# A two-block transformer kernel: modulation accumulations at the end of a feed-forward step, statistic sums shared by POOL and TensorE, a table square root, and the branch scaled on VectorE

## What is computed

```python
def rms_norm(x, g):
    y = x * lax.rsqrt(jnp.mean(x * x, axis=-1, keepdims=True) + EPS)
    return y * g
def modulate(x, g, shift, scale):
    return rms_norm(x, g) * (1 + scale[:, None]) + shift[:, None]
def swiglu(h, w13, w2):
    a, b = jnp.split(h @ w13, 2, axis=-1)
    return (jax.nn.silu(a) * b) @ w2

# first block, layer l: nine modulation vectors from one product
mod = silu(c) @ ada_w[l] + ada_b[l]            # ada_w: [1024, 9 * 1024]
sh1, sc1, g1, sh2, sc2, g2, sh3, sc3, g3 = jnp.split(mod, N_ADA, axis=-1)
h = modulate(x, norm_g[l, 0], sh1, sc1)
x = x + 0.5 * g1[:, None] * swiglu(h, ff_w13[l, 0], ff_w2[l, 0])
...                                            # mixer (hybrid, then NSA), second half feed-forward
# after both layers: rms_norm(x, final_g)

# second block, layer i: a norm before and after each branch
h = rmsnorm(x, g_pre)
f = (silu(h @ w_gate) * (h @ w_up)) @ w_down
x = x + 0.5 * rmsnorm(f, g_post)               # twice; between them
x = x + rmsnorm(mixer(rmsnorm(x, mix_pre)), mix_post)   # conformer convolution, then differential attention
```

## Time and profile before

| | us |
|---|---|
| median of 3 runs | 2526.31 |
| lowest, highest | 2525.79, 2539.52 |
| the profiled execution | 2526.72 |
| its span (first to last instruction) | 2524.9 |
| mean granted TensorE clock | 0.932 of full speed |

### The profile page before, as it was taken

How to read it: one execution, slowest core, us unless ns; L and a number is a source line. 1 busy time by engine, 2 the same in 40 slices (tenths; PEclk the granted TensorE clock), 3 DMA queues, 4 the chain that set the end, 5 groups by cost and what they waited for, 6 DMA issues and landing times.

```text
span 2524.9 us, 41719 instructions
## 1 busy us (share of the span) xinstructions
PE 2252.9 (89%) x17470; PEld 2207.7 (87%) x17470; DVE 1547.4 (61%) x2128; ACT 946.2 (37%) x1209; POOL 113.2 (4%) x68
## 2 busy tenths in 40 slices
PE   2999868898899988989999997978998998987998
PEld 2999868898899988979998997868998998977998
DVE  7666675666766653656447555976556555575654
ACT  2333423333333344433334334224334333434433
POOL 0000000000000000000000001630000000000000
PEclk9999889899999987989998998988998998998999
DMA  6466533466556533114544552213453553411552
GB/s 275 196 256 257 207 139 134 175 250 257 203 227 261 226 137 132 50 51 184 183 167 152 183 182 100 101 40 143 173 192 120 200 183 133 159 59 67 200 182 83
DMA packets 52942, 417.58 MB, mean 165 GB/s; under 512 B 5873, under 2 KB 6001, under 8 KB 6769
## 3 DMA queue, kind: packets, MB, share of 16 engines
q1 hardware_dynamic: 52848, 416.27, 43.9%
HBM read 415.20 MB, written 1.05 MB: 165 GB/s over the span
## 4 chain that ended last, share of the span: by engine, by line
PE 59%; DVE 20%; DMA 10%; ACT 5%; issue 4%; POOL 1%; SPq 1%; DVEq 0%; ACTq 0%
PE AB L259 10%; PE AB L261 10%; PE AB L260 10%; DMA raw<-slabs 10%; DVE ada_acc L1357 7%; PE Y L259 6%; PE Y L260 6%; PE Y L261 6%; DVE lo L1328 4%; ACT hi L954 4%; DVE qT L1903 2%; PE M L524 2%; PE Y L721 2%; PE Y L736 1%; PE M L752 1%
## 5 line engine op out<-in xcount | busy, mean ns | idle before, releaser
L1328 DVE TENSOR_TENSOR lo<-raw,hi 128x2048 fp32r<-128x2048 f32 x322 | 748.5, 2326 | 632.5 <-ACT hi L954 632.3
L259 PE MATMUL AB<-h_hi,hi 128*128 128x256 f32 x3072 | 880.7, 287 | 12.6 <-DVE ada_raw L1913 5.8
L260 PE MATMUL AB<-h_lo,hi 128*128 128x256 f32 x3072 | 875.1, 285 | 0.0
L261 PE MATMUL AB<-h_hi,lo 128*128 128x256 f32 x3072 | 874.8, 285 | 0.0
L954 ACT ACTIVATE hi<-raw 128x2048 fp32r<-128x2048 f32 x322 | 614.6, 1910 | 645.3 <-DMA raw<-slabs 249.2
L259 PEld LDWEIGHTS AB<-h_hi,hi 128*128 128x128 f32 x3072 | 595.8, 194 | 15.3 <-DVE ada_raw L1913 6.8
L260 PEld LDWEIGHTS AB<-h_lo,hi 128*128 128x128 f32 x3072 | 595.9, 194 | 0.1
L261 PEld LDWEIGHTS AB<-h_hi,lo 128*128 128x128 f32 x3072 | 595.4, 194 | 0.0
L259 PE MATMUL Y<-g_hi,hi 128*128 128x256 f32 x1280 | 372.8, 291 | 53.0 <-DVE g_lo L1535 53.0
L261 PE MATMUL Y<-g_hi,lo 128*128 128x256 f32 x1280 | 370.4, 289 | 0.0
L260 PE MATMUL Y<-g_lo,hi 128*128 128x256 f32 x1280 | 370.3, 289 | 0.0
(11 more groups left out here) (291 smaller groups left out, 2274.7 us busy)
## 6 DMA issues: line engine op xcount, KB each, us to landing
raw<-slabs SPq DMA_DIRECT2D x322, 1024.0 KB, 4.8
ada_raw<-ada SPq DMA_DIRECT2D x35, 2048.0 KB, 7.8
x<-x_t SPq DMA_DIRECT2D x1, 1024.0 KB, 10.1
kT<-ada SPq DMA_DIRECT2D x1, 1024.0 KB, 18.4
vt<-ada SPq DMA_DIRECT2D x1, 1024.0 KB, 20.4
out_t<-x SPq DMA_DIRECT2D x4, 256.0 KB, 2.4
vec<-vectors SPq DMA_DIRECT2D x1, 462.0 KB, 3.5
hf<-constants SPq DMA_DIRECT2D x1, 401.0 KB, 15.1
```

Source lines behind the costliest of these rows:

```text
L259: nc.tensor.matmul(out_, w_hi, r_hi, start=start, stop=False, **kw)
L260: nc.tensor.matmul(out_, w_hi, r_lo, start=False, stop=False, **kw)
L261: return nc.tensor.matmul(out_, w_lo, r_hi, start=False, stop=stop, **kw)
L1328: nc.vector.tensor_tensor(lo[slot][:, :], raw[slot][:, :], hi[slot][:, :].bitcast(F32), ALU.subtract).then_inc(lo_done[slot], 1)
```

## The change

Four edits:

1. In VectorE's `step` of a feed-forward, `mod_out` moves behind `gate_lo`, and `mac` becomes the last instruction group of the step, behind the split of A. The order of SP, ScalarE and TensorE in the loop stays.
2. `tree` on POOL makes three additions instead of four; TensorE's `stat_tree` sums chunks 4 and 5 itself and takes them first.
3. A new `deviation` on ScalarE takes `sqrt(M + eps)` with the activation table, and `root_of_sqrt` on VectorE takes its reciprocal and one Newton step. It serves norms 1 to 5, 7 and 10, the final norm and the six additions of the second block. `sqrt_table` runs a small square root on ScalarE at the end of every feed-forward and mixer, before the slabs of `ahead()`.
4. `add(n)` for n >= 6: ScalarE only squares; VectorE scales the branch from PSUM into `hf`, before it takes the root.

```diff
@@ VectorE, step of a feed-forward
                     if not first:
                         split(sb_, i + nb)
+                    split(sw, i + nw)
+                    gate_lo(i + (g0 - 1))
                     if out_:
                         mod_out(i + (q0 - 2))
+                    if a:
+                        split(sa, i + (na + 1))
                     if mac_:
                         mac(0, i + (q0 - 1), i + (a0 - 1))
-                    split(sw, i + nw)
-                    gate_lo(i + (g0 - 1))
-                    if a:
-                        split(sa, i + (na + 1))
@@ TensorE, stat_tree
-                s0, p0 = c.take("sq", KD), c.take("pair", 4)
-                sums([(pair_ready, p0 + 3, sq[:, 0, :]), (pair_ready, p0 + 4, sq[:, 4, :]),
-                      (sq_ready, s0 + 7, sq[:, 6, :]), (sq_ready, s0 + 8, sq[:, 7, :])], ones[1024])
+                s0, p0 = c.take("sq", KD), c.take("pair", 3)
+                sums([(sq_ready, s0 + 5, sq[:, 4, :]), (sq_ready, s0 + 6, sq[:, 5, :]),
+                      (pair_ready, p0 + 3, sq[:, 0, :]), (sq_ready, s0 + 7, sq[:, 6, :]),
+                      (sq_ready, s0 + 8, sq[:, 7, :])], ones[1024])
@@ POOL, tree
-                pool.wait_ge(sq_ready, s0 + 6)
-                nc.gpsimd.tensor_tensor(sq[:, 4, :], sq[:, 4, :], sq[:, 5, :], ALU.add).then_inc(pair_ready, 1)
@@ ScalarE
+            def deviation():
+
+                act.wait_ge(stat_ready, c.take("stat") + 1)
+                nc.scalar.activation(root[:, :], M[:, 0:TT], ACT.Sqrt, bias=eps_[:, 0:1]).then_inc(sqrt_ready, 1)
+
+            def sqrt_table():
+
+                nc.scalar.activation(eps_[:, 1:2], eps_[:, 0:1], ACT.Sqrt)
...
                 g_split(g0 + NSTEP - 1, z_hi)
+                if f >= 4:
+                    c.take("stat")
+                sqrt_table()
                 ahead()
@@ ScalarE, add(n), n >= 6
                             nc.scalar.activation(ysq[:, k, :], Y[:, k, :], ACT.Square, bias=bias).then_inc(sq_ready, 1)
-                        if b == 0:
-                            act.wait_ge(gate_done, n - 5)
-                        for k in (2 * b, 2 * b + 1):
-                            if n == 7:
-                                nc.scalar.activation(hf[:, k, :], Y[:, k, :], ACT.Identity, scale=gate[:, k:k + 1],
-                                                     bias=gate_bias[:, k:k + 1]).then_inc(yg_ready, 1)
-                            else:
-                                nc.scalar.activation(hf[:, k, :], Y[:, k, :], ACT.Copy, scale=gate[:, k:k + 1]
-                                                     ).then_inc(yg_ready, 1)
+                    deviation()
@@ VectorE
+            def root_of_sqrt():
+
+                c.take("stat")
+                vh, tmp = var[:, 0:TT], var[:, TT:2 * TT]
+                dve.wait_ge(sqrt_ready, c.take("sqrt") + 1)
+                nc.vector.tensor_scalar(vh, M[:, 0:TT], EPS, -0.5, ALU.add, ALU.mult).then_inc(dve_link, 1)
+                c.take("link")
+                link(nc.vector.reciprocal(root[:, :], root[:, :]))
+                for t in range(TT):
+                    y = root[:, t:t + 1]
+                    nc.vector.scalar_tensor_tensor(tmp[:, t:t + 1], y, y, vh[:, t:t + 1], ALU.mult, ALU.mult
+                                                   ).then_inc(dve_link, 1)
+                at = c.take("link", TT)
+                for t in range(TT):
+                    y = root[:, t:t + 1]
+                    dve.wait_ge(dve_link, at + t + 1)
+                    nc.vector.scalar_tensor_tensor(y, tmp[:, t:t + 1], 1.5, y, ALU.add, ALU.mult
+                                                   ).then_inc(root_ready, 1)
+                dve.wait_ge(rstd_ready, c["stat"])
@@ VectorE, add(n), n >= 6
-                rstd_of(EPS, copy=False)
                 yg0 = (n - 6) * KD
+                for k in range(KD):
+                    if k % 2 == 0:
+                        dve.wait_ge(sq_ready, SQ_DONE["add", n] - KD + k + 2)
+                    nc.vector.tensor_scalar(hf[:, k, :], Y[:, k, :], gate[:, k:k + 1],
+                                            gate_bias[:, k:k + 1] if n == 7 else None, ALU.mult,
+                                            *([ALU.add] if n == 7 else [])).then_inc(yg_ready, 1)
+                root_of_sqrt()
```

More of the change, by code:

```diff
@@ L146, in program @@
         gate_bias = sb("gate_bias", [P, KD])
+        eps_ = sb("eps", [P, 2])
         ident = sb("ident", [P, P])
@@ L224, in program @@
         o_read = sem("o_read")
-        gate_done = sem("gate_done")
+        sqrt_ready = sem("sqrt_ready")
         yg_ready = sem("yg_ready")
@@ L289, in program @@
                 n_sq += 3
-            if kind == "norm":
-                SQ_DONE[a[0]] = n_sq
+            if kind == "norm" or kind == "add" and a[0] >= 6:
+                SQ_DONE[kind, a[0]] = n_sq
         ADA_FFN = {0: (4, 10), 1: (16, 10), 2: (26, 8), 3: (34, 2)}
@@ L1194, in hybrid @@
                 turn(4, first=4)
+                c.take("stat", 2)
+                sqrt_table()
                 next_slab()
@@ L1368, in begin @@
                 nc.vector.memset(one[:, :], 1.0)
+                nc.vector.memset(eps_[:, :], EPS)
                 for n, t in ones.items():
@@ L1472, in square_sum @@
             def square_sum(n):
-                dve.wait_ge(sq_ready, SQ_DONE[n])
+                dve.wait_ge(sq_ready, SQ_DONE["norm", n])
                 nc.vector.tensor_reduce(rstd[:, :], hf[:, :, :].rearrange("p k t -> p t k"), AXX, ALU.add
@@ L1603, in add @@
                     link(nc.vector.tensor_scalar(gate[:, :], g_src, half, None, ALU.mult))
-                    nc.vector.tensor_tensor(gate_bias[:, :], gate[:, :], v("b_pw2", 0, KD), ALU.mult
-                                            ).then_inc(gate_done, 1)
-                elif n >= 6:
-                    nc.vector.tensor_scalar(gate[:, :], g_src, half, None, ALU.mult).then_inc(gate_done, 1)
+                    link(nc.vector.tensor_tensor(gate_bias[:, :], gate[:, :], v("b_pw2", 0, KD), ALU.mult))
                 else:
```

1 line of the change is left out of this document (added).

## The result

The changed kernel takes 2645.74 us (median; 2642.75 to 2646.7) where the kernel before takes 2526.05 us in runs on the same chip: ratio 1.046, 95% interval 1.042 to 1.049, +119.7 us. The forecast was 2629 us, +102. The profiled execution took 2646.12 us, with a span of 2642.9 us, 118.0 us more than the span of 2524.9 us before.

A forecast was written before the change was run, and what follows sets the result against it. The kernel was taken to be bound in its coupled feed-forward steps by a ring from VectorE's accumulation over SP's loads and the splits. 2526.7 us +132 for the longer ring -30 for the statistics = 2629 us, range 2605 to 2655.

The forecast's parts named there:

- The ring: Coupled feed-forward steps: accumulation, ada_raw issue, slab loads behind it, splits, next accumulation; the move adds 132 us over four feed-forwards.
- The period's terms: Coupled step: 20.5 us plus W's split 2.2, gate_lo 0.6, A's split 2.2, wait 0.3, sequencer 0.1 makes 25.9 us.
- B lands E+10.2: Coupled step: the load of slab B lands 10.2 us after E, the end of an accumulation.
- 0.3 us for `hi` of W: Coupled step: VectorE waits 0.3 us for ScalarE's hi of slab W, counted into the longer period.
- A comes in time, 0.4 us to spare: Coupled step: ScalarE has slab A split by E+17.3, VectorE wants it at E+17.7; a later hi would show it wrong.
- First shift 5.9 us: Start of each feed-forward: the first accumulation comes 5.9 us later, behind W, gate_lo and A.
- Way out -2.5 us: End of each feed-forward's coupled steps: the last part gives back 2.5 us, bounds -4 and 0.
- The statistics: Norms and six additions: root 14.7, tree 5.6 and branch scaling 10.6 less 1.4 for table loads save 30 us, bounds 15 to 40.
- The early table loads: ScalarE's added loads, 1.28 us each, lie where it waits for TensorE; cost 1.4 us; one on the chain would show it wrong.
- the third rival: ScalarE's 16 added table loads lie uncovered, adding 20 us: 2649 us; chance 9%.
- the low clock would hold through the holes: Coupled steps: TensorE's waits keep it at the lower clock, 31.7 us a period, 2741 us in all; chance 4%.
- the ring keeps its length: Coupled steps: some slack takes the added 5.4 us, so only the statistics count: 2497 us; chance 3%.

The follow-up runs named there:

- e1: The kernel before with edit 1 alone (accumulation last in VectorE's step, mod_out behind gate_lo): 2667.16 us, ratio 1.055.
- e3: The changed kernel with SP issuing a step's ada_raw load behind the next step's three slab loads: 2424.78 us, ratio 0.959.
- e2: The changed kernel with VectorE's old order in the step, so edits 2 to 4 alone: 2509.16 us, ratio 0.992.
- e6: The changed kernel without its calls of sqrt_table, so each root loads its table itself: 2637.5 us, ratio 1.042.
- e11: The kernel of e2 (edits 2 to 4 alone) run once more: 2499.39 us, ratio 0.987.
- e10: The kernel of e3 (changed kernel, ada_raw load behind the next step's slab loads) run once more: 2427.65 us, ratio 0.958.
- e9: The kernel of e3 without the early table loads (no calls of sqrt_table): 2419.11 us, ratio 0.956.
- e12: The kernel of e2 without edit 4, so ScalarE, not VectorE, scales the branch; run beside e11: 2511.29 us, ratio 0.993.

## Why the prediction was right, and what was mis-sized

**The ring: right.** The changed kernel and e1 have the waits for `raw<-slabs` 26 us apart, VectorE's accumulation last before SP issues `ada_raw`, no wait for `g_lo` in TensorE's list, and one for `lo` of B in its place (6.0 us each; the text said some 7). e1 is the direct test of the term: the forecast had 132.4 us for all four feed-forwards, and e1's four rows make 47.0+46.9+36.7+2.6 = 133.2. The undoing on SP's side (e3) shows that it was this ring and not the order on VectorE as such: with the late accumulation kept, the slower kernel becomes the fastest.

**The period's terms.** The forecast said 20.5+5.4 = 25.9 us; 26.1 us was measured in e1 and 26.3 in the changed kernel. What the move adds is right: between the end of B's split and the accumulation there are now 5.3 us in both. With E = 194.47, the end of an accumulation in the rows above, the steps come out so:

- "B lands E+10.2": `hi` of B starts at 205.35, E+10.9. This is the mis-sized term: it was read from one step. SP's timeline, before and after:

```profile
207.61 4.47 SPq L418 DMA_DIRECT2D raw<-slabs  x3
```

```profile
195.51 2.25 SPq L419 DMA_DIRECT2D raw<-slabs  x3
```

Before, three slab loads went out within 4.5 us, since the last had to wait for its buffer; after the move all buffers are free by then, and all three go out within 2.3 us. It would be natural to put B's delay down to that, and the forecast had such a bound (0.8 us more "for transfers that queue together"), but e1 rules it out. There the three go out within 1.7 us, and from the second step on `hi` of B starts 10.0 to 10.7 us after the issue of `ada_raw`, 10.3 on average, as in the kernel before (10.1 to 10.5, on average 10.3); in the changed kernel the average is 10.6. B follows the load that stands ahead of it: in nearly every step it lands 2.4 to 2.5 us after `ada_raw`, and W and A each as much behind the slab before, which is 1 MB at the 426 GB/s that were moved from 204.5 to 207.5 (431 from 216 to 219 before). What differs is the 2 MB load itself (tile `ada_raw`, queue of SP, 80 to 245 us: before, e1, e2, changed):

```profile
DMA to landing us min/median/max: 7.6/7.7/8.0
DMA to landing us min/median/max: 7.5/7.6/8.2
DMA to landing us min/median/max: 7.7/7.9/8.2
DMA to landing us min/median/max: 7.9/8.1/8.2
```

The step at E = 206.58 had one of the shortest, 7.6 us, and so a period of 20.5 us where the mean was 20.7; 20.7+5.4 is the 26.1 of e1. The changed kernel's loads took 0.3 us more than those before, and e6, whose SP program is the same, had 7.8 us; why this execution drew slower ones stays open.
- "0.3 us for `hi` of W": 0.25 us (209.84), right. W itself is late with B, and ScalarE waits 0.63 us for it, as before.
- "A comes in time, 0.4 us to spare": `hi` of A ends at 212.25, `lo` starts at 212.72, 0.47 us to spare. Right as a difference; taken by itself, `hi` of A ends at E+17.8, later than the E+17.3 that the forecast had named as a sign of being wrong, because all slabs are late alike.
- First shift 5.9 us: 6.8 us (the first accumulation starts at 83.13 instead of 76.34), since `hi` of A started 0.9 us later than before, behind TensorE.
- Way out -2.5 us: from the last issue of `ada_raw` to the statistic 38.8 us in e1, 42.3 before: -3.4, inside its bounds.

Against the kernel before, the 22 periods are 119.7 us longer in e1 and 123.5 us in the changed kernel, where the forecast had 22x5.4 = 118.8. The later start is offset by the shorter way out. That e1 comes out within 1 us of the forecast is in part such a cancellation.

**Where the missing 17 us are.** By stages the forecast had 132.4 for the ring, less 4x1.75 for root and tree, plus 1.4 for the loads: 126.8 us for the four feed-forwards, and they gave 133.5, 6.7 more. 4.7 of these are the 22 periods. The two mixers gave 9.6 us more than forecast (below), the row "rest" 0.1.

**The statistics: right in sum.** Forecast -30; e2 and e11 gave -21 and -33. The stage "rest", which has no ring and eight of the fourteen roots, should have given 8x1.05 for the roots, 0.7 for the conformer's tree and 10.6 for the branch, 19.7 us; it gave 19.6. The six additions should have given 2.6, 5.0, 3.1, 2.2, 3.2 and 1.1 (root and branch), and gave 2.5, 3.9, 3.5, 2.2, 3.5 and 0.6. The close sum is in part luck: the conformer's 0.7 us did not come (its stage is 0.2 us longer), and four deferred norms gave 1.3 us that nobody had forecast. In the second addition (n = 7) a step of the forecast failed. It let VectorE's eight scalings take 2.7 us and end under the wait for the sum; with their bias they take 3.7 (chain, changed kernel, 1845 to 1856 us):

```profile
1849.98 3.71 DVE hf L1651 x8
1853.70 0.07 DVE var L1478
```

The square root had been ready at 1852.6. From the end of the sum to N there are 2.2 us there, as before, so the root's 1.0 us is lost.

The statistic of norm 1, to be read beside the earlier trace rows (chain, changed kernel, 300 to 345 us):

```profile
337.10 1.51 PE M L525 x12
338.63 0.27 ACT root L982
...
339.00 0.16 DVE var L1478
...
339.87 1.24 PE N L534 x4
```

From the start of the square root (338.63) to N (339.87) there are 1.2 us, where 1.1 were forecast and 2.2 stood before. The sum's x12 take 1.51 us instead of 2.30, but that is no gain of an edit: they are 12 matmuls in both, and e2 needs 1.90 for them.

**The early table loads: off the chain, said the forecast, and that failed.** It priced them at 1.4 us and named a load on the chain as a sign that it was wrong. Seven of twelve are on it. (All loads together are 27, as forecast, against 11 before.) In the four feed-forwards e6 is shorter than the changed kernel by 1.7, 3.4, 2.0 and 2.0 us, 9.1 in all, but that holds the ring's period too. The part that the load can touch runs from the start of `z_hi` to the start of the root: 14.1, 14.1, 13.9 and 15.2 us in the changed kernel, 13.3, 13.3, 13.6 and 14.2 in e6, 2.8 us in all; between e10 and e9, where there is no ring, the same differences are 0.0, 0.8, 0.2 and 0.8, 1.7 in all. So the price there is 1.7 to 2.8 us, with 0.8 to 1.0 us more in each of three additions, and not 20 as the third rival had it. My reasoning asked whether ScalarE was idle around the load; it should have asked who waits for what ScalarE does next. As to the page that the forecast weighed: in the changed kernel `z_hi` ends at 325.17, the load runs from 325.18 to 326.46, and the next activation starts at 326.48. So the drain of 1380 ns, which the Trainium skill (ScalarE: Activation LUTs, What ACT_TABLE_LOAD costs) adds to each switch, does not appear as time here, and the page's figure of 1283 ns for the load does (15.4 us in 12 loads at this line).

**The mixers.** The forecast gave the stages of the two mixers -1.75 us each; they came out at +2.2 and +3.9, 9.6 us above it, the largest part of what it missed. By the pair e3 and e10, and by e2 and e12 in the second mixer (+4.0 us at a granted clock of 0.83 and -3.3 at 0.86, with the same operations there), this is the granted clock of an execution. Whether the changed kernel draws the worse level more often is open: each kernel has few profiles, and the times alone don't show a stage.

**The other rivals.** That the low clock would hold through the holes (2741 us) is out: the holes of 6 us came, and in the stretch from 198.5 to 201.5 the granted clock is 1.00 again. That the ring keeps its length is out by e1.

## What to carry to other kernels

Read a ring by what each queue has standing behind the late instruction, and before moving an instruction, write down the ring for the new order too: what waits for it, what is queued behind that, and where the way back enters. Here an edit that costs 140 us alone and one that is worth nothing alone save 72 to 84 us together, because the queue of loads and the order on VectorE each closed a ring of their own. A transfer time taken from one row is one draw (the 2 MB load took 7.6 to 8.0 us in one feed-forward); a period wants the mean of all rows. A load's time to landing is mostly what stands ahead of it in the queue; and an idle engine around an added instruction does not make it free, unless what follows it there has slack.

## What was not expected of the hardware

A mixer with 670 matmuls had a granted clock of 0.87 in one execution and 0.80 in another of the same kernel, and 8.2 us between them, while the other stages of the two agreed to 0.1 us, but for the first feed-forward (0.4) and two short stages of the hybrid mixer (1.5 and 0.5). A comparison of stages is worth making only when such a stage is set aside.
